# Rests of sixteen gate/up weight chunks: an accumulating transfer in place of a VectorE subtraction

## The chip, the cores and the metric

The kernel runs on one core of one Trainium2 chip. The metric is the device time of one execution in microseconds (us). Before the change three runs gave 1239.83, 1240.52 and 1241.51 us (median 1240.52).

## The reference

Four transformer layers run in a row on one activation of 256 rows and 1024 columns, all in float32: a mixer of dilated attention and a state-space scan, a mixer with a gated linear recurrence, a latent-attention mixer and a grouped-query one. Each is followed by a gated feed-forward unit, and these four units are what the change touches:

```
def swiglu(x, w_gate, w_up, w_down):
    return (jax.nn.silu(x @ w_gate) * (x @ w_up)) @ w_down

x = x + rms_norm(swiglu(rms_norm(x, g), w_gate, w_up, w_down), g2)   # layers 0, 1
x = x + _swiglu(_rmsnorm(x, g), w_gate_up, w_down)                   # layers 2, 3
# x: 256 x 1024, hidden width 2816, gate and up 1024 x 2816 each, down 2816 x 1024
```

## The kernel before, in words

**Weights in chunks.** All weights are packed on the host as an array `in_w` of chunks of 128 partitions x 2048 float32 (1 MB), in the order in which TensorE uses them. SyncE's queue loads each chunk into one of three buffers of `RAW` (chunk n into buffer n mod 3).

**Three products for one.** TensorE multiplies in the type fp32r, to which a float32 is rounded. To keep float32's precision every operand is held as a rounded part and a rest. For a weight chunk ScalarE writes the rounded part (`WH`, line 1199, `split_hi`), and VectorE the rest, `WL = RAW - WH` (line 1838, `split_lo`). Each product is then three matmuls (`mm3`, lines 484 to 486): rounded times rounded, rounded activations times the weights' rests, rests of the activations times rounded weights. `WH` and `WL` have three buffers each as well.

**Order around the change.** Each engine's program is written out by hand, and semaphores tie them:

- `used` counts chunks that TensorE is done with. ScalarE's `feed(c)` (line 1201) rounds chunk c + 3 once chunk c is used, since it goes to c's buffer.
- `hi` counts the chunks rounded, `lo` the rests written. VectorE's `feed` (line 1840) waits for `hi`, and TensorE waits for `lo` ahead of a chunk's first matmul (line 590 and its like).
- SyncE loads chunk c into `RAW` when the rest of chunk c - 3 is written (`weights`, line 2773).

**A gated unit.** Its first 22 chunks hold gate and up weights. A group g (0 to 10) is two of them, `cs[2g]` and `cs[2g+1]`, and gives 256 gate and 256 up columns for both row halves: 24 matmuls of 512 columns for each chunk. Behind group g TensorE transposes the activations of group g - 1 (`fold`, four transposes, line 490). ScalarE and VectorE, on their side, first feed two chunks, then split the transposed activations (`fold`), then evaluate the activation function of group g (`tanh`, line 1311; `gate`, lines 2008 and 2012). For g - 1 = 2, 4, 6 and 8 the `fold` is longer: ScalarE copies a corner to `JK`, VectorE forms five sums (lines 2019 to 2027), and ScalarE goes on when they are done. The remaining 11 chunks of a unit are the down projection.

**GpSimd** does little: small reciprocal roots of the norms, and a few transfers. Between a unit's row norm (`row_rsqrt`) and the norm behind the unit (`post_rsqrt`, or a transfer that waits for the unit's output) its queue holds nothing.

Of the kernel before, what the change touches and what calls it, by code (L numbers as in the profile page):

```python
# [8 lines left out]
NR = 3  # L9
NW = 3  # L10
FAST = (2, 4, 6, 8)
NF = len(FAST)
EV_OUT = (0, 2, 4, 6)
OUT0 = (0, 2, 8, 10, 4, 6)

# [205 lines left out]
class Tally:  # L221
# [14 lines left out]
    w0a w0b w0c w0d hi1 lo1 pa pd pg pp rt rtz dv ev pairs uq rope ropes bhalf bu ang sab trig nr bread bet bbe k0p k0 ch w ssm gy gh gl  # L236
    qk mx ex tp pta ptd pv yt ytp oh ol glua glud
    lama lamd zo zt xg conv cph cpl gt tg odth odaa b4 b1 b2 b3 b8 b9 b10
    sa sf sr tr thi tlo tu ms eo cb
    mt mhi mlo msq hsum kz vm z nz gturn gout ct cth ctl gq kv kpp kpt"""  # L240
Signals = namedtuple("Signals", SIGNALS)

# [13 lines left out]
def program(nc, A, PLAN, NCH):  # L256
# [10 lines left out]
    with top:  # L267
# [190 lines left out]

        TR_ = YG[:, :, :].rearrange("p a (b c) -> p (a b) c", b=2)

        def piece(c):

            return slice(512, CH) if c in FASTS else slice(0, CH)
# [18 lines left out]
        def pe(e):  # L482
# [69 lines left out]
            def edge_rows(cs, per, N, bank, ed):  # L552

                out = PS[:, bank, 0:N]

                def rounded(k):
                    c, w = cs[k // per], slice((k % per) * N, (k % per + 1) * N)
                    if k % per == 0:
                        e.wait_ge(S.lo, c + 4)
                    e.wait_ge(S.hthi, htlo_n(ed, 0, k))  # L560
                    e.matmul(out, HTh[:, k, 0:128], WH[:, c % NW, w], start=k == 0, stop=False)  # L561
                    e.matmul(out, HTh[:, k, 0:128], WL[:, c % NW, w], start=False, stop=False)  # L562

                def rest(k):
                    c, w = cs[k // per], slice((k % per) * N, (k % per + 1) * N)
                    e.wait_ge(S.htlo, htlo_n(ed, 0, k))
                    e.matmul(out, HTl[:, k, 0:128], WH[:, c % NW, w], start=False, stop=k == 7)  # L567

                rounded(0)
                for k in range(8):  # L570
                    if k < 7:
                        rounded(k + 1)
                    rest(k)
                    if k == WHEN[ed]:
                        turn(ed, 1, (0,))
                    elif k == WHEN[ed] + 1:
                        turn(ed, 1, (1,))
# [9 lines left out]
            def rows_mm(cs, per, nkt, N, src, banks, before=None, hook=None, off=0, keep=None, at=None):  # L587
                k = 0
                for ci, c in enumerate(cs):
                    e.wait_ge(S.lo, c + 4)  # L590
                    last = min(k + per, nkt) - 1
                    while k <= last:
                        for t in range(2):
                            if before:
                                before(k, t)
                            w = slice(off + (k % per) * N, off + (k % per + 1) * N)
                            hi, lo, kk = src(k) if callable(src) else (*src, k)
                            tk = product(c, PS[:, banks[t], 0:N], (hi, lo), kk, t, w, k == 0, k == nkt - 1)
                        if k == last:
                            tk.then_inc(keep or S.used, 1)  # L600
                        for fn in at[k] if at and k in at else ():
                            fn()
                        k += 1
                    if hook:
                        hook(ci)

            def fast_chunk(f, ci, c):

                i, m = FAST.index(ci), FASTS[c]
                hi, lo, j = ydst(f, 2 * ci)  # L610
                SFh, SFl = FB[f][6:8]
                W = lambda n: (WH[:, c % NW, 512 * n:512 * n + 512], WL[:, c % NW, 512 * n:512 * n + 512])
                T = lambda n: (TSh[:, n, :], TSl[:, n, :])
                Y = lambda k, t: (hi[:, j + k, 128 * t:128 * t + 128], lo[:, j + k, 128 * t:128 * t + 128])
                S_ = lambda n: (SFh[:, i, 128 * n:128 * n + 128], SFl[:, i, 128 * n:128 * n + 128])

                def mul(b, a, w, own):
                    return mm3(PS[:, b, :], *a, *w, own and i == 0, i == NF - 1)

                def half_sum():  # L620
                    e.wait_ge(S.tlo, 4 * m + 2)
                    if i == 0:
                        e.wait_ge(S.ylo, fold_n(f, 10))
                    mul(4, Y(0, 1), T(0), True).then_inc(S.tu, 1)

                e.wait_ge(S.lo, c + 4)
                tk = mul(5, Y(0, 0), W(1), True)
                if i == NF - 1:
                    tk.then_inc(S.ms, 1)
                e.wait_ge(S.tlo, 4 * m + 1)  # L630
                mul(6, S_(0), T(1), True).then_inc(S.tu, 1)
                if i:
                    half_sum()
                for b, a, w in ((0, Y(1, 0), W(2)), (1, S_(2), W(3))):
                    tk = mul(b, a, w, False)
                    if i == NF - 1:
                        tk.then_inc(S.ms, 1)
                e.wait_ge(S.tlo, 4 * m + 3)
                mul(7, S_(1), T(2), True).then_inc(S.tu, 1)
                if i == 0:  # L640
                    half_sum()
                e.wait_ge(S.tlo, 4 * m + 4)
                mul(2, Y(1, 1), T(3), False).then_inc(S.used, 1)

            def wide_mm(cs, ed, src_of, before, behind=None, at=0, f=None):
# [10 lines left out]
                for ci, c in enumerate(cs[:-2]):  # L656
                    if c in FASTS:
                        before(ci)
                        fast_chunk(f, ci, c)
                        continue  # L660
                    e.wait_ge(S.lo, c + 4)
                    before(ci)
                    for t in range(2):
                        for k in (2 * ci, 2 * ci + 1):
                            tk = both(c, k, t)
                    tk.then_inc(S.used, 1)
                    if ci == at and behind:
                        behind()
                for t in range(2 if ed < 8 else 1):
                    for i in range(4):  # L670
                        c = cs[n - 2 + i // 2]
                        if t == 0 and i % 2 == 0:
                            e.wait_ge(S.lo, c + 4)
                            before(n - 2 + i // 2)
                        if f is not None and i == 0:
                            e.wait_ge(S.cb, 8 * f + 4 * t + 4)
                        if t == 1 and i == 3 and ed < 8:
                            turn(ed, 0)
                        tk = both(c, 2 * n - 4 + i, t)
                        if t == 0 and i == 3:  # L680
                            tk.then_inc(S.half, 1)
                        if t == 1 and i % 2:
                            tk.then_inc(S.used, 1)
# [97 lines left out]

            def glu():
                c = PLAN["glu"][0]
                e.wait_ge(S.lo, c + 4)
                e.wait_ge(S.gl, 1)
                for k in range(4):
                    for m in range(4):
# [211 lines left out]

            def gates(i, bks, free):  # L1000
                c = PLAN[f"rg{i}"][0]
                e.wait_ge(S.lo, c + 4)
                e.wait_ge(S.cpl, i + 1)
                for n in range(4):
                    free(n)
# [189 lines left out]
        def act(e):  # L1195
# [5 lines left out]
            def feed(c, ed=0):  # L1201

                while n_split[0] <= min(c + NW, NCH - 1):
                    n = n_split[0]
                    e.wait_ge((S.w0, S.w1, S.w2)[n % NR], 16 * ((n - 1) // NR + 1))
                    if n >= NW:
                        e.wait_ge(S.used, n - NW + 1)
                    if ed:
                        e.activation(WH[:, n % NW, 0:1024], RAW[:, n % NR, 0:1024], ACT.Copy).then_inc(S.hi2, 1)
                        split_hi(n, slice(1024, CH))  # L1210
# [622 lines left out]
        def dve(e):  # L1833
# [6 lines left out]
            def feed(c, ed=0):  # L1840

                while n_split[0] <= min(c + NW, NCH - 1):
                    n = n_split[0]
                    if ed:
                        e.wait_ge(S.hi2, ed)
                        e.tensor_tensor(WL[:, n % NW, 0:1024], RAW[:, n % NR, 0:1024], WH[:, n % NW, 0:1024].bitcast(f32), SUB)
                    e.wait_ge(S.hi, n + 4)
                    split_lo(n, slice(1024, CH) if ed else piece(n))
                    n_split[0] = n + 1

            def rest(out, src, hi, gain=None):

# [779 lines left out]
        def pool(e):  # L2632
# [25 lines left out]
            def gain_row(i, ed):  # L2658
                e.wait_ge(S.x, x_n(ed, 1, 1))
                e.dma_start(BC[:, :], A["rows"][:, 1024 * i:1024 * i + 1024]).then_inc(S.c_bc, 16)  # L2660

            def mem_rows():
                for t in range(2):
                    e.dma_start(MN[:, t, :], A["mem"][128 * t:128 * t + 128, :]).then_inc(S.c_mem, 16)
# [62 lines left out]
            post_rsqrt(1, 1)  # L2727
            gain_row(2, 1)
            row_rsqrt(1)
            post_rsqrt(2, 0)  # L2730
            post_rsqrt(2, 1)
            gain_row(1, 2)
# [5 lines left out]
            post_rsqrt(3, 1)  # L2738
            gain_row(3, 3)
            row_rsqrt(3)  # L2740
            post_rsqrt(4, 0)
            post_rsqrt(4, 1)
            e.wait_ge(S.x, x_n(4, 1, 1))
# [14 lines left out]
            head_rsqrt("n1", 8)  # L2758
            head_rsqrt("nk1", 8)
            row_rsqrt(5)  # L2760
            e.wait_ge(S.x, x_n(6, 1, 1))
            e.dma_start(tbg[:, :, :, :], A["tab2"][:, 256:768].rearrange("p (c t d) -> p c t d", c=2, t=2)).then_inc(S.c_tb, 16)
            e.dma_start(GRg[:, :, :], A["rows"][:, 4224:4480].rearrange("p (a d) -> p a d", a=2)).then_inc(S.c_gr, 16)
# [3 lines left out]
            head_rsqrt("g1", 8)  # L2767
            head_rsqrt("g3", 8)
            row_rsqrt(7)


        def sync(e):
            def weights(c):
                if c >= NR:
                    e.wait_ge(S.lo, c + 1)
                if c - NR in FASTS:
                    e.wait_ge(S.tr, 4 * FASTS[c - NR] + 4)
                e.dma_start(RAW[:, c % NR, :], A["w"][c]).then_inc((S.w0, S.w1, S.w2)[c % NR], 16)
# [74 lines left out]
```

## Time and profile before

| | |
|---|---|
| median of 3 runs | 1240.52 us (1239.83 to 1241.51) |
| profiled execution | 1240.0 us, of which the profile's span is 1238.2 us |
| TensorE matmuls | 1225.8 us busy, 99% of the span |
| VectorE | 928.7 us busy, 75% |
| ScalarE | 705.9 us busy, 57% |
| GpSimd | 89.3 us busy, 7% |
| HBM read | 214.54 MB, 174 GB/s over the span |

Busy time counts the instructions themselves; an idle engine that nobody waits for costs nothing. Matmul durations overlap (each is some 0.39 us long, and one begins every 0.227 us), so where matmuls are dense TensorE shows as busy without a gap. The times of the views count from the span's start.

### The profile page before, as it was taken

The page shows a single profiled execution, that of the slowest core. Times are in us where ns is not written, and L with a number is a line of the kernel's source. Part 1 is how long each engine was busy: PE and PEld are TensorE (multiplying, and loading weights), DVE is VectorE, ACT ScalarE, POOL GpSimd, SP SyncE. Part 2 cuts the span into 40 slices and gives each one's busy share as a digit, 9 for nine tenths or more (in the row PEclk, how much of TensorE's full clock was granted, in tenths as well). Part 3 has the DMA queues.
Part 4 walks back from the last instruction along what each step waited for, and adds up shares of the span by engine and source line. Part 5 has one row for each costly group of instructions (what it writes and reads, how often), then busy time and mean ns, then how long its engine had stood idle before and what let it go on. Part 6 is the DMA issues. An engine that isn't in the chain of part 4 may idle for free.

```text
span 1238.2 us, 16107 instructions
## 1 busy us (share of the span) xinstructions
PE 1225.8 (99%) x6318; PEld 1021.4 (82%) x6318; DVE 928.7 (75%) x1293; ACT 705.9 (57%) x1065; POOL 89.3 (7%) x121
## 2 busy tenths in 40 slices
PE   7999999999999999999999999999999999999998
PEld 6778888888888888888888888888888888888887
DVE  7995767698788766778887756676888785666787
ACT  7765654455898644455687535444456644544452
POOL 2410000000100100000232000000001300000000
PEclk9999999999999999999999999999999999999999
DMA  8344545555554565555554224545455315555452
GB/s 308 106 137 148 188 171 204 187 187 203 192 201 159 197 213 197 174 189 212 183 200 170 69 103 169 205 170 204 170 204 187 132 35 204 204 173 199 172 183 89
DMA packets 32539, 216.63 MB, mean 175 GB/s; under 512 B 3904, under 2 KB 4544, under 8 KB 7376
## 3 DMA queue, kind: packets, MB, share of 16 engines
q1 hardware_dynamic: 30384, 210.32, 48.6%
q0 software_dynamic: 1360, 4.78, 1.2%
q8 instruction: 50, 0.82, 0.3%
q10 hardware_dynamic: 720, 0.50, 0.1%
q14 instruction: 25, 0.20, 0.1%
HBM read 214.54 MB, written 1.05 MB: 174 GB/s over the span
## 4 chain that ended last, share of the span: by engine, by line
PE 93%; DVE 4%; issue 1%; DMA 1%; ACT 0%; SPq 0%; DVEq 0%; ACTq 0%
PE PS L484 26%; PE PS L486 26%; PE PS L485 26%; PE PS L490 6%; PE PS L860 2%; PE PS L884 1%; PE PS L521 1%; PE PS L519 1%; PE PS L518 1%; PE PS L567 1%; PE PS L562 1%; PE PS L561 1%; DVE WL L1838 1%; DVE YG L2215 1%; DMA X<-in_x 1%
## 5 line engine op out<-in xcount | busy, mean ns | idle before, releaser
L1838 DVE TENSOR_TENSOR WL<-RAW,WH 128x2048 fp32r<-128x2048 f32 (+3 forms) x200 | 434.1, 2174 | 182.3 <-ACT WH L1199 182.3
L1199 ACT ACTIVATE WH<-RAW 128x2048 fp32r<-128x2048 f32 (+3 forms) x200 | 364.4, 1824 | 262.2 <-PE PS L486 262.1
L484 PE MATMUL PS<-WH,HTh 128*128 128x512 f32 (+1 forms) x848 | 334.6, 395 | 0.8 <-DVE WL L1838 0.6
L486 PE MATMUL PS<-WH,HTl 128*128 128x512 f32 (+1 forms) x848 | 329.0, 388 | 0.0
L485 PE MATMUL PS<-WL,HTh 128*128 128x512 f32 (+1 forms) x848 | 328.3, 387 | 0.0
L486 PEld LDWEIGHTS PS<-WH,HTl 128*128 128x128 f32 x848 | 159.2, 188 | 33.3
L484 PEld LDWEIGHTS PS<-WH,HTh 128*128 128x128 f32 x848 | 159.4, 188 | 32.7 <-DVE WL L1838 1.7
L485 PEld LDWEIGHTS PS<-WL,HTh 128*128 128x128 f32 x848 | 159.5, 188 | 30.6
L484 PE MATMUL PS<-WH,YAh 128*128 128x512 f32 x354 | 139.9, 395 | 0.1
L486 PE MATMUL PS<-WH,YAl 128*128 128x512 f32 x354 | 138.0, 390 | 0.0
L485 PE MATMUL PS<-WL,YAh 128*128 128x512 f32 x354 | 137.8, 389 | 0.0
L486 PEld LDWEIGHTS PS<-WH,YAl 128*128 128x128 f32 x354 | 66.4, 188 | 14.0
L484 PEld LDWEIGHTS PS<-WH,YAh 128*128 128x128 f32 x354 | 66.5, 188 | 13.7 <-issue 0.5
L485 PEld LDWEIGHTS PS<-WL,YAh 128*128 128x128 f32 x354 | 66.5, 188 | 13.0
L2635 POOL TENSOR_SCALAR st<-st 128x2 f32<-128x2 f32 (+4 forms) x33 | 21.0, 636 | 752.5 <-ACT JK L1237 679.7
L1216 ACT ACTIVATE YAh<-PS 128x512 fp32r<-128x512 f32 x38 | 21.7, 588 | 58.2 <-DVE JK L2027 29.2
L1216 ACT ACTIVATE HTh<-PS,cst 128x128 fp32r<-128x128 f32 (+1 forms) x136 | 38.8, 380 | 21.9 <-PE PS L490 21.9
L1855 DVE SCALAR_TENSOR_TENSOR HTl<-PS,cst,HTh 128x128 fp32r<-128x128 f32 (+1 forms) x136 | 38.7, 351 | 10.7 <-ACT HTh L1216 10.6
L484 PE MATMUL PS<-WH,YBh 128*128 128x512 f32 x112 | 43.9, 392 | 0.0
L486 PE MATMUL PS<-WH,YBl 128*128 128x512 f32 x112 | 43.6, 389 | 0.0
L485 PE MATMUL PS<-WL,YBh 128*128 128x512 f32 x112 | 43.6, 389 | 0.0
L1854 DVE TENSOR_TENSOR HTl<-YG,HTh 128x512 fp32r<-128x512 f32 x64 | 39.8, 683 | 0.0
(446 smaller groups left out, 1737.6 us busy)
## 6 DMA issues: line engine op xcount, KB each, us to landing
RAW<-in_w SPq DMA_DIRECT2D x196, 1024.0 KB, 4.9
BC<-in_rows POOLq DMA_DIRECT2D x4, 512.0 KB, 4.1
YG<-in_mem POOLq DMA_DIRECT2D x4, 512.0 KB, 5.0
X<-in_x SPq DMA_DIRECT2D x2, 512.0 KB, 5.4
RAW<-in_w SPq DMA_DIRECT2D x4, 256.0 KB, 5.7
BC<-in_s SPq DMA_DIRECT2D x1, 512.0 KB, 11.6
YG<-in_s SPq DMA_DIRECT2D x1, 512.0 KB, 11.9
BB<-in_s SPq DMA_DIRECT2D x1, 512.0 KB, 12.5
```

The source lines that it names most:

```text
L484: e.matmul(out, ah, bh, start=start, stop=False, skip_group_check=joined)
L485: e.matmul(out, ah, bl, start=False, stop=False, skip_group_check=joined)
L486: return e.matmul(out, al, bh, start=False, stop=stop, skip_group_check=joined)
L490: return e.transpose(out, src, ident[0:p, 0:p])
L518: e.matmul(out, HTh[:, k, ts], WH[:, c % NW, w], start=k == 0, stop=False)
L860: tk = e.matmul(PS[:, h % 2, 256 * t:256 * t + 256], q[:, 128 * t:128 * t + 128], k[:, 0:256], start=i == 0, stop=i == len(parts) - 1)
L1199: e.activation(WH[:, c % NW, w], RAW[:, c % NR, w], ACT.Copy).then_inc(S.hi, 1)
L1216: return e.activation(out, src, ACT.Copy, scale=scale)
L1838: e.tensor_tensor(WL[:, c % NW, w], RAW[:, c % NR, w], WH[:, c % NW, w].bitcast(f32), SUB).then_inc(S.lo, 1)
L1854: return e.tensor_tensor(out, src, hi.bitcast(f32), SUB)
L1855: return e.scalar_tensor_tensor(out, src, gain, hi.bitcast(f32), MUL, SUB)
L2635: e.tensor_scalar(st[:, at:at + n], st[:, at:at + n], 1e-6, None, ADD).then_inc(S.var, 1)
```

## The change

`ADDED` names four chunks of each unit, `cs[6]`, `cs[10]`, `cs[14]` and `cs[18]`, sixteen in all. For these

- ScalarE writes the negative of the rounded weights to `WL` (a copy with scale -1) and signals `neg`, and then writes `WH` as ever;
- VectorE does nothing; its count `lo` passes over them, and `lo_n` corrects what others wait for;
- GpSimd waits for `neg` and issues a transfer of the chunk from `in_w` in HBM that adds to what lies in `WL`, which leaves raw minus rounded, the rest. It signals `added`, and each such transfer waits for the one before;
- TensorE waits for `added` in place of `lo`;
- SyncE loads the next chunk into that `RAW` buffer after `hi` in place of `lo`, since nothing but ScalarE reads the buffer.

```diff
+ADDED = (6, 10, 14, 18)
+        ADDS = [PLAN[FFNS[f]][i] for f in range(4) for i in ADDED]
+        def lo_n(c):
+            return c + 4 - sum(a <= c for a in ADDS)
+        def rests_ready(e, c):
+            if c in ADDS:
+                e.wait_ge(S.added, 16 * ADDS.index(c) + 16)
+            else:
+                e.wait_ge(S.lo, lo_n(c))
...
                 for ci, c in enumerate(cs):          # TensorE, rows_mm and its like
-                    e.wait_ge(S.lo, c + 4)
+                    rests_ready(e, c)
...
                     if n >= NW:                      # ScalarE, feed
                         e.wait_ge(S.used, n - NW + 1)
+                    if n in ADDS:
+                        e.activation(WL[:, n % NW, :], RAW[:, n % NR, :], ACT.Copy, scale=-1.0).then_inc(S.neg, 1)
...
                     n = n_split[0]                   # VectorE, feed
+                    n_split[0] = n + 1
+                    if n in ADDS:
+                        continue
...
+            def add_raw(f):                          # GpSimd
+                for c in ADDS[f * len(ADDED):(f + 1) * len(ADDED)]:
+                    n = ADDS.index(c)
+                    e.wait_ge(S.neg, n + 1)
+                    if n:
+                        e.wait_ge(S.added, 16 * n)
+                    e.dma_start(WL[:, c % NW, :], A["w"][c], accum_op=ADD).then_inc(S.added, 16)
...
             row_rsqrt(1)                             # likewise behind row_rsqrt(3), (5) and (7)
+            add_raw(0)
             post_rsqrt(2, 0)
...
             def weights(c):                          # SyncE
-                if c >= NR:
-                    e.wait_ge(S.lo, c + 1)
+                if c - NR in ADDS:
+                    e.wait_ge(S.hi, c + 1)
+                elif c >= NR:
+                    e.wait_ge(S.lo, lo_n(c - NR))
```

On ScalarE, in the first unit, where groups 2 and 3 are fed (`WH<-RAW` rounds a chunk, `JK<-PS` begins the longer fold), there stood before:

```order
L1199 ACTIVATE WH<-RAW 128x2048 [waits s_used,s_w1]
L1199 ACTIVATE WH<-RAW 128x2048 [waits s_used,s_w2]
L1216 ACTIVATE JK<-PS 128x128 [waits s_fold]
L1216 ACTIVATE YAh<-PS 128x512 [waits s_sr]
L1216 ACTIVATE ffn0SFh<-JK 128x384
```

and there stands after the change:

```order
L1212 ACTIVATE WH<-RAW 128x2048 [waits s_used,s_w1]
L1222 ACTIVATE WL<-RAW 128x2048 [waits s_used,s_w2]
L1212 ACTIVATE WH<-RAW 128x2048
L1231 ACTIVATE JK<-PS 128x128 [waits s_fold]
L1231 ACTIVATE YAh<-PS 128x512 [waits s_sr]
L1231 ACTIVATE ffn0SFh<-JK 128x384
```

The write of the negative takes over the wait for `used`; the rounding and the fold come one instruction later.

On GpSimd, between the row norm of the first unit and the norm behind it, there stood before:

```order
L2637 TENSOR_TENSOR st<-st,mh 128x2 [waits s_var]
L2635 TENSOR_SCALAR st<-st 128x1 [waits s_sq]
L2637 TENSOR_TENSOR st<-st,mh 128x1 [waits s_var]
```

and after the change:

```order
L2654 TENSOR_TENSOR st<-st,mh 128x2 [waits s_var]
L2685 DMA WL<-in_w 128x2048 [waits s_neg]
L2685 DMA WL<-in_w 128x2048 [waits s_added,s_neg] x3
L2652 TENSOR_SCALAR st<-st 128x1 [waits s_sq]
L2654 TENSOR_TENSOR st<-st,mh 128x1 [waits s_var]
```

Four transfers stand ahead of the norm behind the unit, each behind two waits.

## Rows read from the trace of the kernel before

**Rows 1.** The page: busy time of the engines, and TensorE's clock in 40 slices.
```profile
PE 1225.8 (99%) x6318; PEld 1021.4 (82%) x6318; DVE 928.7 (75%) x1293; ACT 705.9 (57%) x1065; POOL 89.3 (7%) x121
...
PEclk9999999999999999999999999999999999999999
```
**Rows 2.** The page: shares of the chain that ended last, by engine.
```profile
PE 93%; DVE 4%; issue 1%; DMA 1%; ACT 0%; SPq 0%; DVEq 0%; ACTq 0%
```
**Rows 3.** TensorE's waits, whole span: total us, times, longest.
```profile
PE PS L490 <- DMA ident<-in_tab: 5.1, 1, 5.1
PE PS L529 <- ACT WH L1199: 1.0, 1, 1.0
PE PS L484 <- DVE WL L1838: 0.6, 1, 0.6
```
**Rows 4.** Groups by form: count, busy us, mean ns, idle before.
```profile
L1838 DVE TENSOR_TENSOR WL<-RAW,WH 128x2048 fp32r<-128x2048 f32 x172 | 393.7, 2292 | 174.6 <-ACT WH L1199 174.6
L1199 ACT ACTIVATE WH<-RAW 128x2048 fp32r<-128x2048 f32 x172 | 329.8, 1919 | 242.3 <-PE PS L486 242.2
```
**Rows 5.** Timeline of ScalarE from 171 us: start, duration, instruction, idle before.
```profile
172.48 1.92 ACT L1199 ACTIVATE WH<-RAW 128x2048 fp32r<-128x2048 f32 x1 [3.52 <-PE PS L486]
174.30 0.26 ACT L1216 ACTIVATE JK<-PS 128x128 f32<-128x128 f32 x1
178.20 0.60 ACT L1216 ACTIVATE YAh<-PS 128x512 fp32r<-128x512 f32 x1 [3.65 <-DVE JK L2027]
...
189.73 1.92 ACT L1199 ACTIVATE WH<-RAW 128x2048 fp32r<-128x2048 f32 x1 [2.78 <-PE PS L486]
```
**Rows 6.** Timeline of VectorE, the same place.
```profile
174.43 2.29 DVE L1838 TENSOR_TENSOR WL<-RAW,WH 128x2048 fp32r<-128x2048 f32 x1 [3.15 <-ACT WH L1199]
176.64 0.28 DVE L2019 TENSOR_TENSOR JK<-PS,JK 128x128 f32<-128x128 f32 x1
```
**Rows 7.** Timeline of TensorE at 183 us.
```profile
183.33 0.39 PE L486 MATMUL PS<-WH,HTl 128*128 128x512 f32 x1
183.56 0.60 PE L490 MATMUL PS<-ident,ffn0AN 128*128 128x128 f32 x4
183.92 0.47 PE L484 MATMUL PS<-WH,HTh 128*128 128x512 f32 x1
184.23 0.39 PE L485 MATMUL PS<-WL,HTh 128*128 128x512 f32 x1
```
**Rows 8.** Timeline of GpSimd at 132 us, and landing times of that line's transfers.
```profile
132.06 0.62 POOL L2660 DMA_DIRECT2D BC<-in_rows  x1 [3.02 <-DVE X L1890]
...
DMA to landing us min/median/max: 3.9/3.9/4.8
```
**Rows 9.** Windows: bounds, length, busy of five engines, clock, DMA share, GB/s.
```profile
132.00:133.00 1.00, 1.00 (x8) 0.87 (x7) 0.00 (x0) 1.00 (x4) 0.62 (x1) 1.00 0.00 0
133.00:134.00 1.00, 1.00 (x6) 0.68 (x5) 0.89 (x4) 1.00 (x5) 0.00 (x0) 1.00 0.58 82
```
**Rows 10.** Windows from the earliest data to the deadline (2 of 16, and 2 more).
```profile
153.00:160.92 7.92, 7.92 (x37) 6.50 (x36) 5.54 (x7) 1.92 (x2) 0.00 (x0) 1.00 0.56 206
175.70:183.62 7.92, 7.92 (x37) 6.50 (x36) 6.45 (x16) 3.54 (x5) 0.00 (x0) 1.00 0.38 132
...
781.67:789.59 7.92, 7.92 (x37) 6.50 (x36) 5.53 (x7) 1.92 (x1) 0.00 (x0) 1.00 0.41 136
...
1145.88:1153.80 7.92, 7.92 (x37) 6.50 (x36) 6.52 (x13) 3.54 (x5) 0.00 (x0) 1.00 0.39 132
```
**Rows 11.** The page: DMA queues, with packets, MB and share of 16 engines' span.
```profile
q1 hardware_dynamic: 30384, 210.32, 48.6%
q0 software_dynamic: 1360, 4.78, 1.2%
```
**Rows 12.** One window of Rows 9's kind, in the middle of a chunk's load.
```profile
174.00:175.00 1.00, 1.00 (x6) 0.80 (x5) 0.57 (x1) 0.55 (x2) 0.00 (x0) 1.00 1.02 434
```
**Rows 13.** SyncE's queue: one load of a chunk, and landing times.
```profile
176.75 0.33 SPq L2778 DMA_DIRECT2D RAW<-in_w  x1
...
DMA to landing us min/median/max: 4.7/4.9/11.6
```

More of the change, by code:

```diff
@@ L238 @@
     lama lamd zo zt xg conv cph cpl gt tg odth odaa b4 b1 b2 b3 b8 b9 b10
-    sa sf sr tr thi tlo tu ms eo cb
+    sa sf sr tr thi tlo tu ms eo cb neg added
     mt mhi mlo msq hsum kz vm z nz gturn gout ct cth ctl gq kv kpp kpt"""
@@ L589, in rows_mm @@
                 for ci, c in enumerate(cs):
-                    e.wait_ge(S.lo, c + 4)
+                    rests_ready(e, c)
                     last = min(k + per, nkt) - 1
@@ L624, in half_sum @@
                     mul(4, Y(0, 1), T(0), True).then_inc(S.tu, 1)
-                e.wait_ge(S.lo, c + 4)
+                rests_ready(e, c)
                 tk = mul(5, Y(0, 0), W(1), True)
@@ L660, in wide_mm @@
                         continue
-                    e.wait_ge(S.lo, c + 4)
+                    rests_ready(e, c)
                     before(ci)
@@ L672, in wide_mm @@
                         if t == 0 and i % 2 == 0:
-                            e.wait_ge(S.lo, c + 4)
+                            rests_ready(e, c)
                             before(n - 2 + i // 2)
@@ L783, in glu @@
                 c = PLAN["glu"][0]
-                e.wait_ge(S.lo, c + 4)
+                rests_ready(e, c)
                 e.wait_ge(S.gl, 1)
@@ L1001, in gates @@
                 c = PLAN[f"rg{i}"][0]
-                e.wait_ge(S.lo, c + 4)
+                rests_ready(e, c)
                 e.wait_ge(S.cpl, i + 1)
@@ L1848, in feed @@
                     split_lo(n, slice(1024, CH) if ed else piece(n))
-                    n_split[0] = n + 1
             def rest(out, src, hi, gain=None):
@@ L2740, in pool @@
             row_rsqrt(3)
+            add_raw(1)
             post_rsqrt(4, 0)
@@ L2760, in pool @@
             row_rsqrt(5)
+            add_raw(2)
             e.wait_ge(S.x, x_n(6, 1, 1))
@@ L2769, in pool @@
             row_rsqrt(7)
+            add_raw(3)
         def sync(e):
             def weights(c):
-                if c >= NR:
-                    e.wait_ge(S.lo, c + 1)
+                if c - NR in ADDS:
+                    e.wait_ge(S.hi, c + 1)
+                elif c >= NR:
+                    e.wait_ge(S.lo, lo_n(c - NR))
                 if c - NR in FASTS:
```

## The prediction

> **What bounds the kernel now.** I read the page first: TensorE is busy 99% of the span, at the full clock in every slice [rows 1], and the chain that ended last lies on it for 93% [rows 2]. That says that only time in which TensorE is idle can be won, and that any wait put on it is paid in full. So the next view is TensorE's waits over the whole span: the largest is 5.1 us at the start, and what it waits for VectorE's rests comes to 0.6 us, once [rows 3]. In the stretches of the four units in which gate and up chunks are used, it has no wait at all: the matmuls follow each other every 0.227 us, and the fold's transposes stand between two chunks without a gap [rows 7]. The third view is the timeline of ScalarE and VectorE at a chunk that the change picks, to see what it gives them, and the last one the share of the DMA engines there, since that is what the change draws on.
>
> **VectorE's part.** Sixteen subtractions go, at 2.292 us each [rows 4]: 36.7 us of VectorE. It has 25% idle, and nobody on TensorE's side waits for it in these stretches, so this is worth nothing to the time. At most the 0.6 us of [rows 3] could hang on it, and that lies elsewhere.
>
> **ScalarE's part.** Sixteen writes of the negative come, of the same form as the rounding, 1.92 us each [rows 4]: 30.7 us. Where do they lie? At `cs[10]` of the first unit the rounding begins at 172.48, behind 3.52 us idle; the corner copy follows at 174.30, and then ScalarE stands for 3.65 us until VectorE has formed the sums [rows 5]. VectorE is late with them because it does the subtraction first, from 174.43 to 176.7 [rows 6]. After the change the copy comes at 174.30 + 1.83 = 176.1, VectorE is free, and the sums start then instead of at 176.64. The fold ends about 0.4 us earlier than before. So the 1.92 us fill a hole that the removed 2.29 us had made. At `cs[6]`, where the fold has no sums, ScalarE idles 2.7 us ahead of its next rounding and that is the cover; without it the next rounding would be 1.92 us late, against a deadline two chunks away. Cost on the path: 0. The load of the next chunk into this `RAW` buffer is issued at 176.75 now [rows 13], after the change when the rounding ends, at 172.48 + 2 x 1.92 - 0.1 = 176.2: 0.5 us earlier, worth nothing, and it lies beside the new transfer as before it lay beside nothing.
>
> **GpSimd's part.** Four issues of 0.62 us each a unit [rows 8], on an engine 7% busy [rows 1]. Behind them stands the norm after the unit, which is asked for more than 60 us after the last one. Cost 0. Each also waits for the one before, issued four chunks (22.7 us) earlier: nothing.
>
> **The transfer, the term that decides.** Before, the rest of `cs[10]` was ready 4.3 us after the rounding began. Now it is ready when the transfer has landed. The deadline is the first matmul of `cs[10]`, at 183.92 [rows 7], 11.44 us after ScalarE starts on the chunk; it is the same distance at all sixteen. Of it go:
> - 1.92 us for the negative;
> - about 1.3 us from there to the first data: the transfer issued at 132.06 moves nothing until 133, and is 58% busy in the microsecond behind it [rows 8, 9];
> - about 0.3 us from the last data to TensorE (an estimate: those 0.5 MB landed 3.9 us after issue, and the data took some 2.3).
>
> That leaves 7.92 us, and I laid windows of just that length over the sixteen places. In fourteen of them the DMA engines are 37 to 41% busy with the ordinary load of a chunk; in two, the first of units one and two, 56 and 57% [rows 10]. Free are 7.92 x 0.61 = 4.8 us in fourteen and 7.92 x 0.435 = 3.45 us in two.
>
> How much of the engines' time does one accumulating chunk want? No row shows one; bounds then. Copies of GpSimd's queue took 1.2% of the engines' span for 4.78 MB, that is 0.012 x 1238.2 / 4.78 = 3.1 us a MB or 3.26 us for the 1.049 MB of a chunk; loads of SyncE's queue 0.486 x 1238.2 / 210.3 = 2.86 us a MB, 3.0 us a chunk [rows 11]. In full flow they move 434 GB/s, 2.42 us a chunk [rows 12].
> - Lower end: it costs what a copy does, 3.26 us. It fits everywhere, stall 0.
> - It has to read two inputs, `in_w` and `WL`, for each byte that it writes. If an engine takes them one after the other the price doubles: 6.5 us by the mean rate, 4.8 us by the full-flow rate. By the first TensorE stands 6.5 - 4.8 = 1.7 us fourteen times and 3.1 us twice, 30 us. By the second 0 and 1.4 us twice, 3 us.
> - Upper end: the adder or its small packets are slower than that. Three times a copy, 9.8 us, gives 14 x 5.0 + 2 x 6.3 = 83 us; four times, 13 us, gives 14 x 8.2 + 2 x 9.6 = 134 us.
>
> I take the doubled price, between its two rates: 3 to 30 us, the middle 16 us, or 1 us a chunk. A transfer with company in the engines hides its own latencies, so the mean rate, which holds them, is too dear, and full flow, which no whole transfer reaches, too cheap.
>
> The Trainium skill speaks against the lower end (Collectives: The Full Stack, Part 3, on the bandwidth ceiling): a reduction in the DMA engines is slower not for the addition but because both operands are read through the same ring, and reduce-scatter ran at about half of all-gather. No trace of this kernel shows that yet. Its page on DMA (DMA: Bandwidth & Descriptors, the anatomy of a GpSimd transfer) gives 2.0 us plus bytes over 436 GB/s, 3.2 us for 0.5 MB, where this trace has 3.9 [rows 8]; for a plain copy of a chunk that would be 4.4 us from issue to landing, and the whole change would cost nothing.
>
> **The sum.** The profiled execution took 1240.0 us (span 1238.2 and 1.8 around it), 0.5 below the median of the runs. VectorE 0, ScalarE 0, GpSimd 0, transfer +16: 1256 us. A stall on one chunk is not won back, since TensorE has no idle time behind it, and does not grow into the next, since the next such chunk is 22.7 us away. The ordinary load that shares the engines lands later by up to the new transfer's own time: 176.2 + 4.9 + 6.5 = 187.6, still before its rounding at 189.73 [rows 5].
>
> **Rivals.**
> - *Hidden (chance 0.28).* The two reads overlap, or the adder takes its second input from a port of its own, and a chunk costs under 4.8 us of the engines (3.45 us in two places). Then TensorE never waits: 1240 us, not slower. It decides at that price. For it: loads are bursts, and in the windows 60% of the engines' time is free [rows 10]. Against it: the doubled price passes the mark at every rate but the best.
> - *Dear adder (0.24).* The accumulating transfer costs three times a copy or more; TensorE stands 5 us or more at each of the sixteen, 1240 + 83 = 1323 us, and at four times 1374. For it: nothing in this trace bounds the adder's rate. Against it: at 4 times, 1 MB would move at 80 GB/s, far under all that the rows show.
> - *Faster (0.04).* The rests come late somewhere that I read as not waiting, and a freed VectorE ends it: at most the 0.6 us of [rows 3] and the 1.0 us for ScalarE, 1238.5 us. Against it: neither lies in a unit.
> - My forecast, the doubled price, has 0.44, with its own range of 1243 to 1270.
>
> **How the numbers follow.** A measurement of this kernel tells 0.2% (2.5 us) from no change. Faster by that much: 0.04. Within it: 0.28 of the hidden case and 0.04 of mine at its cheap end, 0.32. Slower: 0.64. The range runs from the hidden case, 1239.5, through mine, to a part of the dear adder, 1308; what it leaves out is the upper half of that case.
>
> **What would show it.** In the profile after: sixteen transfers `WL<-in_w` on GpSimd's queue, whose time to landing is the test. Up to 9.2 us from issue (11.44 - 1.92 - 0.3) TensorE has no wait and I am wrong; at some 10.2 us my sum holds; above 13 the adder is dear. TensorE's waits should show a new row, the first matmul of those chunks released by that transfer, near 1 us each, and larger at the first chunk of units one and two. VectorE should be busy 37 us less, ScalarE 31 us more, with the hole of 3.65 us ahead of the fold cut to about 1.3. The forecast also fails if TensorE waits for `fold` or for ScalarE in the units.

## The result and the profile after

The changed kernel takes 1249.82 us (median of 4 runs, 1248.84 to 1251.36) where the kernel before takes 1240.45: a ratio of 1.0077, 95% interval 1.0065 to 1.0089. It is slower by some 9.4 us. The profiled execution took 1250.68 us, its span 1248.9, 10.7 more than before.

The page of the changed kernel (busy time, then the chain that ended last, by engine, then the queues as in [rows 11]):

```profile
PE 1229.9 (98%) x6318; PEld 1023.3 (82%) x6318; DVE 893.4 (72%) x1277; ACT 734.7 (59%) x1081; POOL 103.3 (8%) x137
...
q1 hardware_dynamic: 30384, 210.32, 47.7%
q0 software_dynamic: 3664, 21.56, 8.6%
...
PE 86%; DVE 5%; DMA 5%; ACT 2%; issue 1%; POOL 1%; SPq 0%; DVEq 0%; ACTq 0%
...
WL<-in_w POOLq DMA_DIRECT2D x16, 1024.0 KB, 9.3
```

VectorE lost 35.3 us of work, ScalarE gained 28.8, and neither moved the end. The chain, which held 1% of transfers before [rows 2], now holds 5%. The sixteen new transfers land 9.3 us after their issue.

TensorE's waits answer to [rows 3]; under them the landing times of the new transfers, shortest, median and longest:

```profile
PE PS L497 <- DMA WL<-in_w: 6.1, 5, 2.5
PE PS L503 <- DMA ident<-in_tab: 5.1, 1, 5.1
PE PS L542 <- ACT WH L1212: 1.0, 1, 1.0
...
DMA to landing us min/median/max: 9.1/9.3/11.9
```

A new row stands at the top. Only the stalls that the view could name are in it. Set against the kernel before, matmul by matmul (there are 6318 in both, in one order), TensorE's start times slip by 8.3 us at the sixteen first matmuls of the added chunks: 2.6 and 2.8 us at the first one of units one and two, and 2.95 us at the fourteen others together. Of these fourteen four lost 0.3 to 0.8 us each and ten 0.13 us or less. Another 2.0 us had slipped by 132 us, before the first of these chunks: 0.6 us while the first weights load, and 1.4 us more net over a stretch of 3.4 us at half the granted clock (more on it at the end). The two runs with a full mean clock took 1248.84 and 1248.95 us, so these 1.4 us belong to this execution and not to the change. The last 0.4 us is almost all one wait of the transposes at 680 us for VectorE, outside the units; it stands in the kernel without transfers too, and why it comes is open. (The expectations below count these steps at 8.7 us.)

The place that the forecast worked out, `cs[10]` of the first unit, in the timelines of ScalarE, GpSimd, SyncE's queue and TensorE (it begins at 177.06 now, at 172.48 before):

```profile
177.06 1.92 ACT L1222 ACTIVATE WL<-RAW 128x2048 fp32r<-128x2048 f32 x1 [3.53 <-PE PS L499]
178.88 1.90 ACT L1212 ACTIVATE WH<-RAW 128x2048 fp32r<-128x2048 f32 x1
180.68 0.25 ACT L1231 ACTIVATE JK<-PS 128x128 f32<-128x128 f32 x1
182.54 0.60 ACT L1231 ACTIVATE YAh<-PS 128x512 fp32r<-128x512 f32 x1 [1.61 <-DVE JK L2044]
```
```profile
179.28 0.87 POOL L2685 DMA_DIRECT2D WL<-in_w  x1 [24.31 <-ACT WL L1222]
```
```profile
180.80 0.33 SPq L2809 DMA_DIRECT2D RAW<-in_w  x1
```
```profile
188.15 0.60 PE L503 MATMUL PS<-ident,ffn0AN 128*128 128x128 f32 x4
189.23 0.50 PE L497 MATMUL PS<-WH,HTh 128*128 128x512 f32 x1 [0.49 <-DMA WL<-in_w]
```

The negative takes 1.92 us, the rounding and the corner copy follow, and ScalarE's hole ahead of the fold shrinks from 3.65 us [rows 5] to 1.61; the fold's copy comes 5.48 us after the chunk's start, 5.72 before. The transfer is issued at 179.28, the load that shares the engines 1.5 us later. The first matmul, which stood directly behind the transposes before [rows 7], starts 0.76 us late. In windows (columns as in [rows 9]) the DMA engines, before 56% busy at the first place of the unit and 38% at the second [rows 10], are full at both:

```profile
157.20:165.50 8.30, 6.29 (x30) 5.00 (x28) 3.88 (x5) 4.26 (x4) 0.00 (x0) 1.00 1.01 303
180.90:188.90 8.00, 7.84 (x37) 6.31 (x35) 6.47 (x15) 4.08 (x7) 0.00 (x0) 1.00 0.96 250
```

### The profile page after: what moved, and what is told of

It reads as the page before. It is cut to its first block, busy times and chain, and to the rows that moved or that the text cites. A ratio compares the mean times of both kernels' runs of the same rounds, so it can differ in the third digit from the quotient of the medians.

```text
span 1248.9 us, 16138 instructions
## 1 busy us (share of the span) xinstructions
PE 1229.9 (98%) x6318; PEld 1023.3 (82%) x6318; DVE 893.4 (72%) x1277; ACT 734.7 (59%) x1081; POOL 103.3 (8%) x137
## 4 chain that ended last, share of the span: by engine, by line
PE 86%; DVE 5%; DMA 5%; ACT 2%; issue 1%; POOL 1%; SPq 0%; DVEq 0%; ACTq 0%
PE PS L497 24%; PE PS L499 23%; PE PS L498 23%; PE PS L503 5%; DMA WL<-in_w 4%; PE PS L873 2%; PE PS L897 1%; DVE WL L1853 1%; PE PS L534 1%; PE PS L532 1%; PE PS L531 1%; PE PS L580 1%; PE PS L574 1%; PE PS L575 1%; ACT WL L1222 1%
## 5 line engine op out<-in xcount | busy, mean ns | idle before, releaser
L1853 DVE TENSOR_TENSOR WL<-RAW,WH 128x2048 fp32r<-128x2048 f32 (+3 forms) x184 | 397.1, 2162 | 145.1 <-ACT WH L1212 145.1
L497 PEld LDWEIGHTS PS<-WH,YAh 128*128 128x128 f32 x354 | 66.5, 188 | 13.7 <-issue 0.5
L1222 ACT ACTIVATE WL<-RAW 128x2048 fp32r<-128x2048 f32 x16 | 30.7, 1917 | 54.8 <-PE PS L499 54.8
L2036 DVE TENSOR_TENSOR JK<-PS,JK 128x128 f32<-128x128 f32 x16 | 4.6, 289 | 61.3 <-ACT JK L1231 61.3
L1872 DVE SCALAR_TENSOR_TENSOR HTl<-PS,cst,HTh 128x128 fp32r<-128x128 f32 (+1 forms) x136 | 38.7, 351 | 10.7 <-ACT HTh L1231 10.6
```

Source lines behind the costliest of these rows:

```text
L497: e.matmul(out, ah, bh, start=start, stop=False, skip_group_check=joined)
L1222: e.activation(WL[:, n % NW, :], RAW[:, n % NR, :], ACT.Copy, scale=-1.0).then_inc(S.neg, 1)
L1853: e.tensor_tensor(WL[:, c % NW, w], RAW[:, c % NR, w], WH[:, c % NW, w].bitcast(f32), SUB).then_inc(S.lo, 1)
L1872: return e.scalar_tensor_tensor(out, src, gain, hi.bitcast(f32), MUL, SUB)
```

## The experiments

The theory: the change costs what the landing of a transfer passes TensorE's deadline by. The issue comes 2.22 us after ScalarE's start on the chunk, so of the 11.44 us some 9.2 are left from issue to landing. The landing is long because a transfer that adds takes the DMA engines nearly twice as long as a copy, and because ordinary loads share them. Rivals: ScalarE's longer way, a gain of VectorE's that hides in the sum, GpSimd's way of issuing, the second reading of HBM. The times are set against runs of the kernel before that were taken beside them.

**Without the transfers.**

```diff
-                e.wait_ge(S.added, 16 * ADDS.index(c) + 16)
+                e.wait_ge(S.hi, c + 4)
-            add_raw(0)                        # and 1, 2, 3
```

> ScalarE writes the negative of the sixteen chunks and VectorE leaves out their rests, but no transfer adds the raw weights, and TensorE waits for the rounding alone; the rests of these chunks are left out of the result (the negative of the weights stands in their place). Theory (the whole cost is the wait for the transfer): 1240.5 us, the time before, within 1 us, and TensorE without a wait in the units. Rival (part of the 9 us is ScalarE's longer way to the fold, or a fold that comes late): 1243 us or more, with waits for ScalarE. Second rival (a relieved VectorE is worth something by itself, and the transfer ate it): 1238 us or less.

Measured: 1241.23 us (10 runs), ratio 1.0006, 0.9997 to 1.0016. TensorE's waits hold no row in the units. This kernel leaves the rests of the sixteen chunks out. Matmul by matmul TensorE loses nothing at the sixteen places, and the five runs with a full mean clock have a median of 1240.21 us, the kernel before at that clock 1239.98. So neither the sixteen writes of ScalarE nor the sixteen subtractions less are seen in the time. Both the rival of a late fold and that of a hidden gain fall: the whole loss hangs on the transfer, and the prize would have been nothing.

**A copy in place of the addition.**

```diff
-                    e.dma_start(WL[:, c % NW, :], A["w"][c], accum_op=ADD).then_inc(S.added, 16)
+                    e.dma_start(WL[:, c % NW, :], A["w"][c]).then_inc(S.added, 16)
```

> The sixteen transfers copy the raw weights to WL in place of adding them (so WL holds raw weights, not rests); all waits as in the change. Theory (the price is the second input that an adding transfer reads): packets of 8 KB take some 309 ns as in SyncE's loads instead of 629, landing falls from 9.3 us to about 6 to 6.5, under the 9.25 that the deadline leaves from the issue, and the time is 1240.5 us. Rival (it is GpSimd's way of issuing, or sharing the engines with the loads, whatever the transfer does): landing stays above 8.5 us and the time above 1246 us.

Measured: 1240.89 us (10 runs), ratio 1.0009, 1.0000 to 1.0019. The queue's share and the landing times:

```profile
q0 software_dynamic: 3664, 21.56, 5.3%
...
DMA to landing us min/median/max: 5.1/5.2/8.2
```

TensorE loses nothing at any of the sixteen places (the rests are wrong here: `WL` holds the raw weights). The same bytes out, on the same queue, behind the same waits, landed in 5.2 us instead of 9.3, with the middle packet of 8 KB at 325 ns instead of 629. The engines' time for one transfer comes out of the shares: (5.3 - 1.2)% of 1240.4 us over 16 is 3.2 us for a copy, (8.6 - 1.2)% of 1248.9 over 16 is 5.8 us for an addition, 1.8 times as much. GpSimd's queue and the company of the loads by themselves are not to blame. Of the 4.1 us a small part does lie ahead of the data: the issue took 0.53 us instead of 0.86, and the first data came 1.22 us after its start instead of 1.57. Those 0.35 us are small beside 4.1, but more than any of the ten places with the least loss lost (0.13 us).

**The load behind it held back.**

```diff
                 if c - NR in ADDS:
                     e.wait_ge(S.hi, c + 1)
+                    e.wait_ge(S.added, 16 * ADDS.index(c - NR) + 16)
```

> The change, but the ordinary load into the RAW buffer of an added chunk, which is issued 1.5 us behind the transfer and shares the engines with it, waits until the transfer has landed. Theory (5.8 us of engine time each for the transfer, and the load's 3 us on top, make the landing of 9.3 us): landing 7.3 us in the middle places, about 8.5 us at the first chunk of units one and two, which have one more load in the engines; stalls gone or nearly, 1240.5 to 1242 us. Rival (the adder alone sets the landing): landing still above 9 us and the time 1249 us. Risk in either: the held load comes too late for its own rounding, seen as a wait of ScalarE for the load; in the middle places it would land some 3 us ahead of it.

Measured: 1241.84 us (10 runs), ratio 1.0016, 1.0006 to 1.0026; landing times

```profile
DMA to landing us min/median/max: 7.8/8.1/9.4
```

The kernel is 1.8 us over the kernel before, so 7.6 of the 9.4 us are gone. The landing fell by 1.2 us, less than the 2.0 that I had expected, but enough to pass under the deadline at fourteen places; at the two worst it came after 9.4 us (I had said 8.5), and TensorE lost 0.2 us at each. Two things fell: the data ended after 7.6 us instead of 8.5, and landing followed them by 0.3 us instead of 0.6. So the shared engines matter, and the addition alone does not decide; it makes the margin thin. The risk came true once: ScalarE waited 3.5 us for a held load, and TensorE, two chunks away, did not notice.

**Without the first chunk of each unit.**

```diff
-ADDED = (6, 10, 14, 18)
+ADDED = (10, 14, 18)
```

> The change for cs[10], cs[14] and cs[18] alone; the first chunk of each unit is split by VectorE again. Theory (of 8.7 us of steps in TensorE's time against before, those four places hold 2.5 + 2.9 + 0.3 + 0.8 = 6.5 us): 1249 - 6.5 = 1242.5 us, with the stalls of the twelve others as they were. Rival (stalls are of the same size at all sixteen, so a quarter of 8.7 goes): 1246.7 us.

Measured: 1243.66 us (6 runs, 1242.60 to 1245.01), ratio 1.0030, 1.0018 to 1.0041. Three runs lie at 1242.6 to 1242.8, as expected, three at 1244.5 to 1245.0. In the profiled one, of the slower three, the first transfer landed after 10.8 us, and TensorE lost 1.6 us there where the change lost 0.8. The four first places cost most, and the rival of equal stalls (1246.7) is out. A landing near the deadline differs from run to run: in this profile every one of the twelve but the last passed it, and they cost 4.1 us where they had cost 1.8 in the change's.

**At the two worst places alone.**

```diff
-        ADDS = [PLAN[FFNS[f]][i] for f in range(4) for i in ADDED]
+        ADDS = [PLAN[FFNS[f]][6] for f in range(2)]
...
-                for c in ADDS[f * len(ADDED):(f + 1) * len(ADDED)]:
+                for c in ADDS[f:f + 1]:
```

> The change at two places alone, the first chunk of units one and two, where one more load is in the DMA engines and the landing was 11.7 and 11.9 us. Theory (the stalls add up place by place): 2.5 + 2.9 = 5.4 us over the kernel before, 1245.6 us, with landing near 11.8 us at both. Rival (the long landings come of GpSimd's queue having other transfers before or behind, or of the sum of all sixteen): under 1243 us.

Measured: 1246.45 us (5 runs, 1244.61 to 1251.38), ratio 1.0053, 1.0035 to 1.0072. Two transfers of sixteen cost 6.2 us, two thirds of the loss; the lowest run, the one with a full mean clock, is 4.4 us over the kernel before. The expected 5.4 lie between, and part of the spread is the clock (last section). In the profiled run, the slowest, TensorE's starts slipped by 3.7 and 2.1 us at the two places:

```profile
PE PS L497 <- DMA WL<-in_w: 5.3, 2, 3.4
...
DMA to landing us min/median/max: 11.3/12.1/12.9
```

At these two, loads were issued 4.4 and 2.2 us ahead of the transfer and a third one 1.5 us behind it; at the first chunks of units three and four it was 5.7 and 3.4 us ahead. Their longer landing is theirs and no matter of the other fourteen; that it comes from the load 2.2 us ahead is argued from these positions, since no run moved that load.

**Added from RAW in place of HBM** (with the load held, as above, since `RAW` is read to the end).

```diff
-                    e.dma_start(WL[:, c % NW, :], A["w"][c], accum_op=ADD).then_inc(S.added, 16)
+                    e.dma_start(WL[:, c % NW, :], RAW[:, c % NR, :], accum_op=ADD).then_inc(S.added, 16)
```

> As e3 (the load behind is held until the transfer has landed), but the transfer adds the chunk from RAW in SBUF instead of in_w in HBM. Theory (an engine takes both inputs one after the other, wherever they lie): packets stay at 629 ns, landing 7.8 us as in e3, 1241 to 1242 us, and HBM reads fall back to 214.5 MB. Rival (the second reading of HBM makes the price): packets near 309 to 450 ns and landing under 7 us. Second rival (two inputs from SBUF's DMA side get in each other's way): landing above 9 us, time up.

Measured: 1241.66 us (10 runs), ratio 1.0010, 1.0000 to 1.0019.

```profile
q0 software_dynamic: 3664, 21.56, 7.9%
HBM read 214.54 MB, written 1.05 MB: 174 GB/s over the span
...
DMA to landing us min/median/max: 6.9/7.1/10.4
```

The middle packets stayed at 629 to 644 ns although nothing was read from HBM: (7.9 - 1.2)% of 1241.5 us over 16 is 5.2 us for one. So the second input costs nearly its full time wherever it lies; HBM's part is at most the 0.6 us between 5.8 and 5.2, and 1.0 us of the landing (7.1 against 8.1 with the load held). The rival of a price made by the second reading of HBM falls.

**A narrow input.**

```diff
-                    e.dma_start(WL[:, c % NW, :], A["w"][c], accum_op=ADD).then_inc(S.added, 16)
+                    e.dma_start(WL[:, c % NW, :], A["narrow"][:, :], accum_op=ADD).then_inc(S.added, 16)
...
+        "narrow": np.zeros((128, 2048), dtype=__import__("ml_dtypes").bfloat16),
```

> The change, but the sixteen transfers add a bf16 array of zeros, 4 KB a partition, in place of 8 KB of float32 (so the rests hold the negative of the rounded weights). Theory A (the price is bytes read: 8 KB of WL and 4 KB of the other): packets of about 309 + 155 = 460 ns, landing some 7.5 us. Theory B (the price is the adder's, by elements): packets stay at 629 ns and landing at 9.3 us. Time 1240.5 to 1243 us by A, 1249 us by B.

Measured: 1243.22 us (one run), just above theory A's range and far from B's 1249;

```profile
q0 software_dynamic: 3664, 21.56, 7.2%
...
DMA to landing us min/median/max: 6.7/6.7/10.9
```

With the elements unchanged and three quarters of the bytes read, a transfer takes (7.2 - 1.2)% of 1241.4 over 16, 4.7 us: bytes alone would say 0.75 x 5.8 = 4.3, elements alone 5.8. The landing fell to 6.7, further than the 7.5 that I had expected. The middle packet lay between 479 and 628 ns from transfer to transfer, so the price goes mostly by the bytes. What the rest is stays open; the narrow input is also converted to another type on its way, and that was not tried apart.

**In halves.**

```diff
+                        for h in range(2):                     # ScalarE
+                            w = slice(1024 * h, 1024 * h + 1024)
+                            e.activation(WL[:, n % NW, w], RAW[:, n % NR, w], ACT.Copy, scale=-1.0).then_inc(S.neg, 1)
...
+                    for h in range(2):                         # GpSimd
+                        w, sem = slice(1024 * h, 1024 * h + 1024), (S.added, S.added2)[h]
+                        e.wait_ge(S.neg, 2 * n + h + 1)
...
+                        e.dma_start(WL[:, c % NW, w], A["w"][c, :, w], accum_op=ADD).then_inc(sem, 16)
...
+                        if c in ADDS and k % per == 2:          # TensorE
+                            e.wait_ge(S.added2, 16 * ADDS.index(c) + 16)
```

> The change with each of the sixteen transfers in two halves of 1024 columns, each behind its half of the negative; TensorE waits for the second half only ahead of the chunk's 13th matmul, 2.7 us later. Theory (TensorE stands because the whole landing, 9.3 us from the issue, passes a deadline of 9.25 us): the first half is issued 1 us earlier and lands by about 6 to 7 us, the second has 12 us and lands at some 10; no stall in fourteen places, and at most 0.5 us in the first ones of units one and two: 1240.5 to 1242 us. Rival (two issues and twice as many descriptors cost what they win): 1246 us or more.

Measured: 1243.90 us (6 runs), ratio 1.0030, 1.0017 to 1.0042. The time lies between theory and rival: 6.0 us of 9.4 are gone. TensorE lost 0.2 to 0.9 us at five places, all at the second half, whose data ended up to 12.2 us after its issue. By then a second ordinary load, issued 8 to 10 us behind, was in the engines as well. That it is the reason is not shown: the other eleven second halves had such a load too and landed after 9.9 to 11.8 us.

**In halves, with the load held back.** Both edits together; the load waits for the second half.

> Both mends together: halves as in e5, and the load behind an added chunk held until its second half has landed as in e3. Theory: TensorE has no wait for a transfer at any of the sixteen places, as when there was no transfer (e1), so 1240.1 to 1241 us, and no gain over the kernel before, since nothing that TensorE waits for was VectorE's. Rival (the held load comes late for its rounding, ScalarE waits for it and TensorE behind it): 1243 us or more.

Measured: 1240.84 us (10 runs, 1240.54 to 1242.10), ratio 1.0004, 0.9995 to 1.0013. TensorE loses nothing at the sixteen places; ScalarE once waits 3.4 us for a held load. This is the time of the kernel before: the transfer can be hidden, and nothing is won by it.

**Eight chunks of each unit.**

```diff
-ADDED = (6, 10, 14, 18)
+ADDED = (6, 8, 10, 12, 14, 16, 18, 20)
```

> The change on eight chunks of each unit (6, 8, 10 to 20), 32 in all, with nothing held or halved. Theory (each place pays by itself what its landing passes 9.25 us by; the next transfer is 11.3 us behind, so it does not queue): the sixteen places of the change pay their 8.7 us again, the sixteen new ones, which share the engines with one load each, 0.1 to 0.3 us each: 1251 to 1254 us. Rival (the transfers and loads start to queue behind each other, as the DMA engines near 80% busy): landing grows from transfer to transfer and the time goes over 1262 us. VectorE falls by another 37 us and wins nothing.

Measured: 1270.69 us (4 runs, 1267.63 to 1273.01), ratio 1.0248, 1.0231 to 1.0265.

```profile
q0 software_dynamic: 5968, 38.34, 15.4%
...
PE PS L497 <- DMA WL<-in_w: 20.6, 12, 3.2
...
DMA to landing us min/median/max: 9.1/9.8/13.1
```

My sum of places was wrong, by 17 us, and the rival's number right, though its picture only half: the landing does not grow from transfer to transfer, it jumps between 9.1 and 13. Thirteen of the 32 landed after more than 10.6 us. At four of them a load had been issued 0.3 to 2 us ahead of the transfer, whose first data then came after 2 to 4.4 us instead of 1.6; two are the known worst places; at the other seven no load was issued so close ahead, and why these landed late is open. A queue forms too: five times the transfer before had not landed in time, and GpSimd issued 0.2 to 1.9 us late. In the timelines a stall shifts the engines' programs against each other, and I read it that a stall can so breed the next one once they are 11 us apart instead of 23; no run shows that apart.

## Why the prediction was right, and where its sizes were off

- **What bounds the kernel.** Right. TensorE had no idle time to give, and the wait put on it was paid in full: the 8.3 us of steps were never won back, and the two runs at full clock are 8.4 and 8.5 us over the kernel before. That VectorE's 37 us are worth nothing is shown by the kernel without transfers (1.0006).
- **ScalarE's and GpSimd's part at 0.** Right: ScalarE's by the same run and by the fold, which came 0.24 us earlier where I had said 0.4; GpSimd's by the plain copy, which keeps its issues and waits (1.0009).
- **The deadline of 11.44 us.** Right at the sixteen places. Its parts were off: I gave 1.3 us from the negative to the first data, and it was 0.3 us to the issue and 1.57 from there (2.1 at the two worst places); 0.3 us from the last data to TensorE, and it was about 0.7 (data to 8.5 us, landing at 9.2 to 9.3, TensorE 0.04 us later). Both ends ate 0.9 us of the window that I had laid. With the load held back, landing follows the data by 0.3 us, so nearly all of the second miss is the load's.
- **The doubled price.** The term that decided, and right in kind: 5.8 us of the engines for a chunk, where I had 4.8 and 6.5 as bounds. The Trainium skill's rule (Collectives: The Full Stack, Part 3: both operands of a reduction go through one ring, so it takes twice as long) agrees with the packets, 629 ns against 325, and with a price that stays when the input comes from SBUF.
- **The sharing.** Too dear. I counted the load's whole 3.0 us against the window. Holding it back won 1.2 us of landing: packets of both queues are under way in an engine at once, and the share of busy time counts each in full (windows of 1 us show shares of 1.12 and 1.15 at 156 and 159 us of the changed kernel). With this the fourteen ordinary places paid 2.95 us in all, where the middle of my bounds gave about 12.
- **The two worst places.** I gave them 1.4 to 3.1 us each by the 56% in the windows; they paid 2.6 and 2.8. The size of the whole, +16, was off for the ordinary ones: measured +9.4.
- **Partly luck.** With the measured price of 5.8 us my way of counting gives 14 x (5.8 - 4.8) + 2 x (5.8 - 3.45) = 19 us, and with the 0.9 us lost at the window's ends 33; measured are 8.3. The load that I counted in full takes up the difference, so the middle of 16 us lay nearer than its parts. That the two worst places are later than the rest was seen ahead and holds by itself (5.4 of the 8.3 us). Whether the fourteen others would wait hung on a few tenths of a microsecond. The sign that I had named, a landing of some 10.2 us and waits near 1 us each, did not come: the median landing was 9.3, against a limit of 9.2, and ten places lost 0.13 us or less.
- **A stall on one chunk does not reach the next.** At 23 us apart nothing speaks against it. At 11 us the sum of places fails by 17 us.
- **The hidden case** (0.28) needed a price of under 4.8 us for a chunk; the price was above it, the landing was 9.3 against 9.2, and holding one load back nearly brings the case about (+1.8 us), halving as well does (1.0004). The dear adder and the faster case fall.
- The Trainium skill's formula for a plain copy of GpSimd's (DMA: Bandwidth & Descriptors, 2.0 us plus bytes over 436 GB/s, 4.4 us a chunk) is short of the copy measured beside a load, 5.2 us. By it the whole change was to cost nothing, and with a plain copy it costs 0.8 us (1.0009).

## What to carry to other kernels

Before work is taken off an engine, ask who waits for it; here nobody did, and 37 us less of VectorE were worth nothing even with the transfer hidden. In this kernel a transfer that adds cost the DMA engines 1.8 times a copy (5.8 us against 3.2), and it starts late by the time its first operand takes to be written, so measure its landing against the consumer's deadline and look which loads are issued near it (here one, 1.5 us behind it). Where it is close, first hold the load that can wait: that alone gave back 7.6 of 9.4 us with one line, cutting the transfer in halves 6.0.

## What the runs showed of the hardware

**A wait of TensorE can cost twice.** In the kernel with the two worst places alone TensorE stood for 3.44 us at the first and 1.86 us at the second. Its timeline, and windows of 1 us behind the first (the granted clock is the number ahead of the DMA share):

```profile
162.95 0.60 PE L503 MATMUL PS<-ident,ffn0AN 128*128 128x128 f32 x4
166.98 0.50 PE L497 MATMUL PS<-WH,HTh 128*128 128x512 f32 x1 [3.44 <-DMA WL<-in_w]
...
461.62 0.64 PE L497 MATMUL PS<-WH,HTh 128*128 128x512 f32 x1 [1.86 <-DMA WL<-in_w]
```
```profile
166.70:167.70 1.00, 0.72 (x3) 0.63 (x4) 1.00 (x2) 0.99 (x2) 0.00 (x0) 1.00 0.95 401
167.70:168.70 1.00, 1.00 (x6) 0.78 (x5) 0.89 (x3) 0.15 (x1) 0.00 (x0) 0.79 1.06 238
168.70:169.70 1.00, 1.00 (x4) 0.81 (x3) 0.96 (x3) 0.00 (x0) 0.00 (x0) 0.50 0.55 213
169.70:170.70 1.00, 1.00 (x3) 0.79 (x3) 0.73 (x5) 0.00 (x0) 0.00 (x0) 0.50 1.01 426
...
171.70:172.70 1.00, 1.00 (x6) 0.82 (x5) 0.00 (x0) 0.00 (x0) 0.00 (x0) 1.00 0.02 8
```

About 1.3 us after TensorE goes on, the granted clock falls from 2.4 to 1.2 GHz for 3.4 us, in which matmuls start every 0.43 instead of 0.23 us: some 1.6 us more on top of the stall. It happened at both places of this execution; at the second the clock fell 0.2 us after TensorE went on. It happened at neither of the two in the changed kernel's, where TensorE stood for 2.27 and 2.52 us. In the kernel with eight chunks a unit the clock fell once, 1.5 us behind an idle time of 1.97 us, and did not fall behind idle times of 2.94 and 3.24 us. So the length of the idle time alone does not decide it. It explains a part of the spread of this kernel's runs (1244.61 with a mean granted clock of 1.000, 1251.38 with 0.996).

**The same fall without a stall.** In the changed kernel's profile it stands at 66 us, ahead of any added chunk:

```profile
66.00:67.00 1.00, 1.00 (x4) 0.77 (x5) 1.00 (x2) 1.00 (x2) 0.92 (x3) 0.59 0.00 0
67.00:68.00 1.00, 1.00 (x4) 0.81 (x3) 1.00 (x2) 1.00 (x3) 0.27 (x1) 0.50 0.01 4
```

The profiles of five of the experiments hold it at the same place (without transfers, plain copy, load held, from RAW, two worst places), and the kernel before's and the five others do not. In the six that hold it the full clock had begun 14.3 to 15.0 us into the span, in the six others 12.5 to 13.7 us in; more is not shown of why it comes. Of 21 runs of the kernel before, beside the experiments with halves and narrow input, 7 have a mean clock of 0.998 or 0.999 and take 1241.2 to 1241.9 us, the 14 others 1239.6 to 1240.8. That these 7 hold the same fall is likely by the size and not shown, since they have no profile. It costs 1.4 us, and has to be taken off before changes of 0.1% are judged.

**Packets of an adding transfer.** The median packet of 8 KB takes 629 ns where a copy's takes 325 on the same queue; the issue itself takes GpSimd 0.86 us instead of 0.53.
